# Attention in a two-block float32 network on one Trainium2 core: scores of both key heads issued together, two pairs ahead, and read out of PSUM in a single VectorE pass

## What is computed

```python
s_loc = einsum('bnqhgd,bnkhd->bnhgqk', qb, kw) * scale    # blocks of 128 queries, 3 blocks of keys
s_loc = where(abs(k_pos - q_pos) <= 128, s_loc, -inf)
s_ctx = einsum('bqhgd,bkhd->bhgqk', qb, k_ctx) * scale      # 256 context keys
p = softmax(concat([s_loc, s_ctx, sink]))[..., :-1]
o = p_loc @ v_loc + p_ctx @ v_ctx
```

## Time and profile before

| | us |
|---|---|
| median of 3 runs | 4574.9 (4571.43 to 4575.47) |
| the profiled execution, span from its first to its last instruction | 4582.2 |
| TensorE matmul busy in it | 4136.4 (90%) |
| VectorE busy | 1514.1 (33%) |
| ScalarE busy | 815.7 (18%) |
| GpSimd busy | 399.9 (9%) |
| attention, from 3317.4 to 3500.2 us of the span | 182.8 |

### The profile page before, as it was taken

How to read it: one execution, slowest core, us unless ns; L and a number is a source line. 1 busy time by engine, 2 the same in 40 slices (tenths; PEclk the granted TensorE clock), 3 DMA queues, 4 the chain that set the end, 5 groups by cost and what they waited for, 6 DMA issues and landing times. The chain is left out here.

```text
span 4582.2 us, 42779 instructions
## 1 busy us (share of the span) xinstructions
PE 4136.4 (90%) x14694; PEld 2260.8 (49%) x14694; DVE 1514.1 (33%) x3325; ACT 815.7 (18%) x1818; POOL 399.9 (9%) x385
## 2 busy tenths in 40 slices
PE   6789999998888999999999996998799889999984
PEld 4466666666433444444444443545665344444432
DVE  4577777776340000000000004235854310000003
ACT  2223333332110000000000003111164100110002
POOL 0111111111000000000000000002500010000001
PEclk8889999998988999999999998998789989999987
DMA  7111111111558888888888874010021179999986
GB/s 284 37 28 36 41 37 41 34 33 29 196 203 341 306 312 309 308 307 308 310 308 310 310 266 148 28 32 5 3 108 65 64 280 335 336 332 338 334 308 231
DMA packets 437207, 875.36 MB, mean 191 GB/s; under 512 B 89746, under 2 KB 134626, under 8 KB 430922
## 3 DMA queue, kind: packets, MB, share of 16 engines
q1 hardware_dynamic: 410905, 785.79, 49.2%
q0 software_dynamic: 19616, 71.38, 4.6%
q10 hardware_dynamic: 6544, 16.39, 0.9%
HBM read 801.07 MB, written 72.43 MB: 191 GB/s over the span
## 5 line engine op out<-in xcount | busy, mean ns | idle before, releaser
L1743 PE MATMUL moe_gbank<-moe_ring,moe_xT 128*128 128x512 f32 x1536 | 681.0, 596 | 3.8 <-ACTq L1799 3.8
L1761 PE MATMUL moe_acc<-moe_ring,moe_hidT 128*128 128x512 f32 x1536 | 675.1, 592 | 1.8 <-DVEq L1860 1.1
L1743 PE MATMUL moe_ubank<-moe_ring,moe_xT 128*128 128x512 f32 x1536 | 675.1, 592 | 0.0
L1833 DVE TENSOR_TENSOR moe_hid<-moe_sg,moe_ubank 128x512 f32<-128x512 f32 x96 | 66.0, 687 | 1636.5 <-PE moe_ubank L1743 1636.5
L791 PE MATMUL gdn_pbank<-first_xT,mix_w 128*128 128x512 f32 (+1 forms) x1280 | 540.4, 557 | 4.3 <-PEq L688 4.3
L1743 PEld LDWEIGHTS moe_gbank<-moe_ring,moe_xT 128*128 128x128 f32 x1536 | 293.8, 191 | 374.4 <-issue 371.2
L1761 PEld LDWEIGHTS moe_acc<-moe_ring,moe_hidT 128*128 128x128 f32 x1536 | 288.2, 190 | 347.1 <-issue 347.1
L1743 PEld LDWEIGHTS moe_ubank<-moe_ring,moe_xT 128*128 128x128 f32 x1536 | 284.5, 190 | 322.4 <-issue 322.4
L1804 ACT ACTIVATE moe_sg<-moe_gbank 128x512 f32<-128x512 f32 x96 | 57.3, 597 | 1548.7 <-PE moe_gbank L1743 1548.7
L791 PEld LDWEIGHTS gdn_pbank<-first_xT,mix_w 128*128 128x128 f32 x1280 | 230.1, 194 | 167.9 <-issue 162.4
L2188 PE MATMUL proj_abank<-mix_yT,mix2x_wq 128*128 128x512 f32 x416 | 180.8, 592 | 0.6 <-PE proj_abank L2188 0.6
(11 more groups left out here) (540 smaller groups left out, 4781.4 us busy)
## 6 DMA issues: line engine op xcount, KB each, us to landing
moe_ring<-in_moe_w_gate SPq DMA_DIRECT2D x64, 2048.0 KB, 7.9
moe_ring<-in_moe_w_up SPq DMA_DIRECT2D x64, 2048.0 KB, 8.7
moe_ring<-in_moe_w_down SPq DMA_DIRECT2D x64, 2048.0 KB, 7.9
moe_ring<-in_w_gate SPq DMA_DIRECT2D x32, 2048.0 KB, 9.2
moe_ring<-in_w_up SPq DMA_DIRECT2D x32, 2048.0 KB, 10.0
moe_ring<-in_w_down SPq DMA_DIRECT2D x32, 2048.0 KB, 9.8
front_wt<-in_w_mod SPq DMA_DIRECT2D x24, 1024.0 KB, 12.7
mix_w<-in_gdn_w_in SPq DMA_DIRECT2D x32, 512.0 KB, 4.1
```

What stands on the lines that cost most here:

```text
L1743: last = nc.tensor.matmul(bank[:], xT[:, k, :], w[:, k * 512:(k + 1) * 512], start=(k == 0), stop=(k == KD - 1))
L1761: last = nc.tensor.matmul(acc[j][:], hidT[:, k, :], w[:, k * D + j * 512:k * D + (j + 1) * 512], start=(f == 0 and k == 0), stop=(f == NF ...
L1833: nc.vector.tensor_tensor(hid[:], sg[:], ubank[:], ALU.mult).then_inc(u_free, 1)
```

## The change

Five things change, all in `attention`:

1. `scores(n, step)` issues one of 6 steps of a **pair**: steps 0 and 1 are two heads of context scores of both key heads (4 products, key heads 0 and 1 in turn), steps 2 to 5 one head of latent scores of both (2 products). Bank 0 of `cbank` and `lbank` belongs to key head 0, bank 1 to key head 1.
2. Scores run two pairs ahead. All of pairs 0 and 1 is issued ahead of the first transpose; pair n + 2 is issued in the first unit of pair n, one step after each transposed tile and what is left behind the last. `sc` has 6 buffers.
3. Both evictions are done by VectorE with `tensor_tensor_reduce`: add a table and take the row maximum in one pass. `band` now holds 0 and -1e30, and for context scores the table is `none`, all zeros. ScalarE's `context` and the separate reduction over the unit are gone.
4. VectorE's `maxima(n)` is for a pair; it stands between `reciprocals(2n)` and `divide(2n)`.
5. ScalarE does `exponentials(u + 1)` ahead of the tile copies of unit u.

```diff
-                def scores(u):
...
-                    part = slice(kv * HD, (kv + 1) * HD)
-                    for pair in range(2):
-                        if ncx >= 2:
-                            pe.wait_ge(c_free, ncx - 1)
...
-                    for g in range(QPK):
-                        if nl >= 2:
-                            pe.wait_ge(l_free, nl - 1)
+                def scores(n, step):
+                    parts = [slice(kv * HD, (kv + 1) * HD) for kv in range(KVH)]
+                    if step < 2:
+                        if 2 * n + step:
+                            pe.wait_ge(c_free, KVH * (2 * n + step))
+                        for g in (2 * step, 2 * step + 1):
+                            for kv, part in enumerate(parts):
+                                last = nc.tensor.matmul(cbank[kv][:, (g % 2) * LC:(g % 2 + 1) * LC], qT[part, g, n * P:(n + 1) * P], kT[part, 0:LC], start=True, stop=True)
                         last.then_inc(c_full, 1)
+                    else:
+                        g = step - 2
+                        lo, cnt, _ = window(n)
+                        if QPK * n + g:
+                            pe.wait_ge(l_free, KVH * (QPK * n + g))
+                        for kv, part in enumerate(parts):
+                            last = nc.tensor.matmul(lbank[kv][:, 0:cnt * P], qT[part, g, n * P:(n + 1) * P], kT[part, LC + lo * P:LC + (lo + cnt) * P], start=True, stop=True)
+                        last.then_inc(l_full, 1)
+                for n in range(AHEAD):
+                    for step in range(STEPS):
+                        scores(n, step)
                 for u, (n, kv) in enumerate(units):
                     pe.wait_ge(p_ready, u + 1)
+                    steps = iter(range(STEPS) if kv == 0 and n + AHEAD < NT else ())
                     for c in kt:
...
-                    if u + 2 < len(units):
-                        scores(u + 2)
+                        for step in itertools.islice(steps, 1):
+                            scores(n + AHEAD, step)
+                    for step in steps:
+                        scores(n + AHEAD, step)
...
+                def maxima(n):
+                    for half in range(2):
+                        dve.wait_ge(c_full, 2 * n + half + 1)
+                        for kv, (x, stat) in enumerate(pair):
+                            for g in (2 * half, 2 * half + 1):
+                                last = V.tensor_tensor_reduce(out=x[:, g, 0:LC], in0=cbank[kv][:, (g % 2) * LC:(g % 2 + 1) * LC], in1=none[:], scale=1.0, scalar=-BIG,
+                                                              op0=ALU.add, op1=ALU.max, accum_out=stat[:, CMAX_, g:g + 1])
+                            last.then_inc(c_free, 1)
+                    for g in range(QPK):
+                        dve.wait_ge(l_full, QPK * n + g + 1)
+                        for kv, (x, stat) in enumerate(pair):
+                            V.tensor_tensor_reduce(out=x[:, g, LC:LC + cnt * P], in0=lbank[kv][:, 0:cnt * P], in1=band[:, b0:b0 + cnt, :].rearrange("p b k -> p (b k)"), scale=1.0, scalar=-BIG,
+                                                   op0=ALU.add, op1=ALU.max, accum_out=stat[:, LMAX_, g:g + 1]).then_inc(l_free, 1)
```

More of the change, by code:

```diff
@@ L1 @@
+import itertools
 import math
@@ L2577, in attention @@
         rb = st.sb("rb", [P, 2, P])
-        lbank = [st.ps(f"lbank{i}", [P, 512]) for i in range(2)]
-        cbank = [st.ps(f"cbank{i}", [P, 512]) for i in range(2)]
+        lbank = [st.ps(f"lbank{i}", [P, 512]) for i in range(KVH)]
+        cbank = [st.ps(f"cbank{i}", [P, 512]) for i in range(KVH)]
         tbank = [st.ps(f"tbank{i}", [P, 512]) for i in range(2)]
@@ L2667, in _, with exponentials @@
             def _(act):
-                def context(u):
-                    if u >= RING:
-                        act.wait_ge(t_full, tiles_before(u - RING + 1))
-                    for pair in range(2):
-                        act.wait_ge(c_full, 2 * u + pair + 1)
-                        nc.scalar.activation(sc[u % RING][:, 2 * pair:2 * pair + 2, 0:LC], cbank[pair][:].rearrange("p (g k) -> p g k", g=2), ACT.Copy).then_inc(c_free, 1)
-                ntr = 0
-                context(0)
-                context(1)
-                for u, (n, kv) in enumerate(units):
-                    _, cnt, _ = window(n)
+                def exponentials(u):
+                    _, cnt, _ = window(units[u][0])
                     x, stat = sc[u % RING], stats[u % RING]
@@ L2686, in _ @@
                     last.then_inc(p_ready, 1)
+                exponentials(0)
+                for u, (n, kv) in enumerate(units):
+                    if u + 1 < len(units):
+                        exponentials(u + 1)
                     if u:
                         act.wait_ge(o_full, u)
-                    for c in range(NC_T + cnt):
-                        act.wait_ge(t_full, ntr + 1)
-                        nc.scalar.activation(pT[:, c, :, :].rearrange("p g k -> p (g k)"), tbank[ntr % 2][:], ACT.Copy).then_inc(t_free, 1)
-                        ntr += 1
@@ L2693, in _ @@
-                    if u + 2 < len(units):
-                        context(u + 2)
+                    ntr = tiles_before(u)
+                    for c in range(NC_T + window(n)[1]):
+                        act.wait_ge(t_full, ntr + c + 1)
+                        nc.scalar.activation(pT[:, c, :, :].rearrange("p g k -> p (g k)"), tbank[(ntr + c) % 2][:], ACT.Copy).then_inc(t_free, 1)
             @block.vector
             def _(dve):
-                nc.vector.memset(band[:, 1, :], BIG)
+                nc.vector.memset(band[:, 1, :], 0.0)
@@ L2714, in maxima @@
                     dve.drain()
-                    nc.vector.tensor_reduce(stat[:, MAX_, :], x[:, :, 0:LC + cnt * P], AX.X, ALU.max)
+                    for x, stat in pair:
+                        V.tensor_tensor(stat[:, CMAX_, :], stat[:, CMAX_, :], stat[:, LMAX_, :], ALU.max)
                     dve.drain()
-                    nc.vector.scalar_tensor_tensor(out=stat[:, LMAX_, :], in0=stat[:, MAX_, :], scalar=SC, in1=snk[:, kv * QPK:(kv + 1) * QPK], op0=ALU.mult, op1=ALU.max)
+                    for kv, (x, stat) in enumerate(pair):
+                        V.scalar_tensor_tensor(out=stat[:, LMAX_, :], in0=stat[:, CMAX_, :], scalar=SC, in1=snk[:, kv * QPK:(kv + 1) * QPK], op0=ALU.mult, op1=ALU.max)
```

64 lines of the change are left out of this document (28 added, 36 removed).

## The result

The changed kernel takes 4584.14 us (median of 12 runs, 4577.84 to 4590.85) where the kernel before takes 4574.04 (12 runs, 4565.14 to 4584.72): a ratio of 1.0022, 95% interval 1.0013 to 1.0031. It is slower, as forecast, but by 10 us and not by 35: 4584 lies under the range of 4590 to 4640. In the profiled execution (span 4583.2 us) attention goes from 3317.6 to 3507.8 us, 190.2 long; before it took 182.8. The rest of the program, which the change does not touch, differs by 6 us between the two profiled executions (4399.4 and 4393.0), so only attention is compared by them.

What follows compares the result with a forecast made beforehand. TensorE's own list was taken to bound attention before, a chain of score round trips after the change. Attention's parts, +26.9 us, and the clock, +8.5, make +35.4 on the median 4574.9: forecast 4610 us, range 4590 to 4640.

Steps and rivals of the forecast that it cites:

- start: Attention before its first transposes: scoring all of pairs 0 and 1 puts these at 36.0 instead of 14.6 us, +21.4.
- pair 0: First pair of attention: half clock until its value product, 29.0 us against 25.8, +3.2.
- pairs 1 to 4 at full clock: Interior pairs of attention: 24.0 us each instead of 21.84, +8.6 in all.
- falls of the clock: Late in first units, behind the second context step: clock falls until the value product, 1.7 us in five pairs, +8.5.
- pair 5: Pair of attention whose scores are for the narrower pair 7: 22.4 us, +0.6.
- pairs 6 and 7: End of attention: pair 6 has no scores left, 14.0 us against 20.3, -6.3; pair 7, -0.6.
- the price of the fused pass: VectorE's evictions of scores: 0.52 us for 256 elements and 0.655 for 384, including 0.08 for the statistic.
- My lower end: Fused pass 0.08 us cheaper than priced: kernel at 4601 us, or 4593 without the fall of the clock.
- The faster rival: Attention: round trips hide and TensorE's own work bounds, 18.2 us a pair, kernel at 4554 us; chance 0.06.
- the fills: Score products until they reach VectorE: 1.00 us for a latent step, 1.3 for a context step, at full clock.
- the halves at once: Score products of key heads 0 and 1 run together on TensorE's array halves: 4.3 us less streaming a pair.
- The rivals on the halves and on half clock throughout: Halves not running at once: 4643 us, chance 0.02; half clock through every first unit: 4634 us, chance 0.12.

Runs made afterwards that it cites:

- drained version: The changed kernel with a drain of VectorE ahead of every fused pass; 4613.1 us, ratio 1.0079 to the kernel before.
- c2_spread3: `b4_best3` with a unit's three steps behind its first, third and last tile instead of first, second and third; 4545.5 us, ratio 0.9935 to the kernel before.
- split version: The changed kernel with a semaphore count for each key head, so each product waits for its own bank alone; 4570.52 us, ratio 0.9988 to the kernel before.
- added waits: The changed kernel with one more, already satisfied semaphore wait ahead of each fused pass; 4589.0 us, ratio 1.0027 to the kernel before.
- b2_fused_alone: The kernel before with the fused pass alone, its order, unit-wise scores and waits kept; 4572.78 us, ratio 0.9997 to the kernel before.
- b4_best3: The changed kernel with steps in both units, one and a half pairs ahead, per-head counts and a later setup wait; 4558.09 us, ratio 0.9968.
- b1_same_half: The changed kernel with both key heads' score products contracted over partitions 0 to 63; 4583.58 us, ratio 1.0025, later stages getting other data.

## Why the prediction was wrong in size and right in kind

| step | forecast us | measured |
|---|---|---|
| start | +21.4 | +16.1 |
| pair 0 | +3.2 | -3.2 |
| pairs 1 to 4 at full clock | +8.6 | -0.3 |
| falls of the clock | +8.5 (five of 1.7) | +3.3 (two of 1.64) |
| pair 5 | +0.6 | -1.6 |
| pairs 6 and 7 | -6.9 | -7.0 |
| together | +35.4 | +7.4 |

The rows are rounded each for itself. The medians differ by 10.1, attention in the two traces by 7.4; the runs' spread is larger than what lies between.

**The step that failed is the price of the fused pass**, "so nothing for the second operation and 0.08 for the statistic: 0.52 and 0.655 us". It measured 0.345 and 0.48 from start to start, 0.175 less. At the 114 passes counted that is 20.0 of the 28 us missing; the other 8 are the clock, below. It closes the single terms too: the start, 36.0 less 30 passes at 0.175, is 30.8, as measured; a first unit with its value product, 17.0 less 14 at 0.175, is 14.6, measured 14.83. The drained version, which restores the forecast's spacing nearly (0.55 and 0.69), restores the forecast's stage: 219.7 us against 218.2. That they agree so closely is in part luck, since its pair 0 took 3 us less than forecast and its pairs 1 to 4 over 4 us more. Both durations were right. The error was to add them, and to take a duration, or a spacing with a wait in it, for the spacing of passes that wait for nothing. My lower end, 0.08 cheaper, was the duration alone, and so too high as well. The row that had the answer stood in the earlier trace rows: two plain passes of 256 elements in 0.76 us. The faster rival named 0.28 as its turning point; at 0.345 the kernel lies near it, which is why so little is left.

The page Vector Engine (DVE) Microarchitecture Reference of the Trainium skill, section Measured stream behaviour on trn2, gives 1.0417 ns an element and some 75 ns an instruction in a stream of them. By that rule I estimate a pass at 0.342 and 0.475 us, and the traces agree (0.345 and 0.48). I had not weighed it. Of the two rules that I had weighed, both from the page TensorEngine Tiling (Array Packing) of the Trainium skill, the one against the change (section PSUM Bottleneck) held for the change itself. It is no bound: `c2_spread3` empties every bank with VectorE alone, in less time than the rival built on the other rule (4545.5 against 4554).

**The clock** is the second miss, and the other 8 us. Of five falls forecast in pairs 1 to 5 two came, in pairs 3 and 4, each at the forecast price, at the end of the stretch behind the second context step where it was placed (0.76 from 3424 to 3431). With passes 0.2 us further apart three of four interior first units lost it, and in the split version none, which looks like fewer falls with shorter gaps. But with the added waits, whose gaps are 0.1 longer, one unit lost it and not two, and each count is from one execution; what decides between near cases is not shown. Pair 0 was to stay at half clock until its value product, but the clock was back 2.4 us behind the first transposes (0.51 from 3348.36 to 3350.80, 1.00 from there to 3361.00), and fell for 3.4 us in the value product: some 3 of the 6.4 us by which pair 0 was forecast too long, and 2.5 are passes. I had read from the earlier trace rows that transposes and scores do not bring the clock back; here they did. In the order of before they did as well, in `b2_fused_alone`, 4.5 us behind the first transposes (0.50 from 3327.65 to 3332.10, 1.00 from there on), where in the trace of the kernel before it took 15.2. So the 3.2 us that pair 0 gained here are not shown to be the change's own.

**Right** were the chain itself, the fills (1.02 against 1.0; 1.24 and 1.3), the halves at once, the second unit (6.93 against 7.0), pairs 6 and 7, and that nothing is gained from ScalarE. The rivals on the halves and on half clock throughout did not happen.

## What to carry to other kernels

Price a run of instructions on one engine by the distance between starts where nothing is waited for, and look for such a pair even at another place: in the trace before, the first two plain passes of the stage stood 0.34 us apart and lasted 0.42 each, and two small VectorE operations stood 0.08 us apart and lasted 0.16 each. When a change turns alternating banks into a joint fill and a joint eviction, count the round trips, and put into each of them as much of the waiting engine's own work as it lasts; where the steps stand among the tiles was worth 15 us here (`b4_best3` to `c2_spread3`: attention 165.2 to 150.3, ratios 0.9968 and 0.9935), more than the whole effect of the change. Moving work further ahead or nearer is settled by the place it takes in each engine's list, not by whether its length fits.

## What I had not expected of the hardware

A reading of the accumulator started in the same 10 ns as the next fused pass (3323.02), and a satisfied semaphore wait between two passes left their overlap as it was, while a drain cost 0.2 us. And in `b1_same_half` the clock fell in every first unit, with TensorE busy 24.7 of 27.1 us in one of them, at 0.62: in the whole of attention it was busy 235.4 of 273.3 us, 86%, at a granted clock of 0.68, where in the changed kernel 143.2 of 190.2 us, 75%, went with 0.90. The busy share of a stretch alone does not tell which clock it gets.
